# First block: two half-empty weight tiles joined, gate tiles moved behind the preparation, three pairs' logits between the last tiles

## What is computed

```python
h = rms_norm(x, g_pre)
a_q, a_kv, a_g, b_cq, b_ckv, b_kr, c_q, c_kv, z = split_cols(h @ w_in)
o_a = nsa_attention(a_q, a_kv, a_g, cmp_pos, cmp_w1, cmp_w2, rel_bias[:4])   # compressed, selected, window; gates a_g
q_full = concat(q_nope, rope(q_rope))  from  rms_norm(b_cq, q_norm) @ w_uq
k_full = concat(k_nope, rope(b_kr))    from  rms_norm(b_ckv, kv_norm) @ w_ukv
o_b = causal_block_attention(q_full, k_full, v)
o_c = banded_attention(c_q, c_k, c_v, 128, rel_bias[4:], sinks)
mixed = concat(o_a, o_b, o_c) * silu(z)
x = x + rms_norm(mixed @ w_out, g_post)
```

## Time and profile before

| | us |
|---|---|
| median of three runs (2575.82 to 2582.0) | 2581.92 |
| the profiled execution, its own time | 2581.8 |
| its span, first to last instruction | 2580.0 |
| first layer's tiles 6 to 23 with the preparation | 51.4 to 177.4 |
| second layer's tiles 6 to 23 with the preparation | 366.5 to 492.9 |

### The profile page before, as it was taken

How to read it: one execution, slowest core, us unless ns; L and a number is a source line. 1 busy time by engine, 2 the same in 40 slices (tenths; PEclk the granted TensorE clock), 3 DMA queues, 4 the chain that set the end, 5 groups by cost and what they waited for, 6 DMA issues and landing times. The chain is left out here.

```text
span 2580.0 us, 35090 instructions
## 1 busy us (share of the span) xinstructions
PE 2469.5 (96%) x13238; PEld 1980.9 (77%) x13238; DVE 1294.1 (50%) x1920; ACT 661.1 (26%) x1331; POOL 654.4 (25%) x510
## 2 busy tenths in 40 slices
PE   8999999999699999999999999899999999999997
PEld 6866778667588888788788888788887887788885
DVE  5547565574633343787533334433345776533344
ACT  3126330263211100643311100311102533311101
POOL 2005510164233311101433311333312002333311
PEclk9989999999899999999999999999999999999998
DMA  6400132000322322221222331222321312223322
GB/s 256 136 32 18 50 133 86 25 18 17 105 98 97 101 101 84 91 75 58 77 95 97 110 106 66 91 98 94 111 97 65 107 51 74 83 96 98 115 98 77
DMA packets 58666, 224.83 MB, mean 87 GB/s; under 512 B 6404, under 2 KB 8596, under 8 KB 58300
## 3 DMA queue, kind: packets, MB, share of 16 engines
q1 hardware_dynamic: 54288, 208.96, 24.5%
q10 hardware_dynamic: 4268, 14.33, 1.5%
HBM read 221.14 MB, written 5.80 MB: 88 GB/s over the span
## 5 line engine op out<-in xcount | busy, mean ns | idle before, releaser
L172 DVE CAST two_hi<-two_raw 128x1024 fp32r<-128x1024 f32 (+1 forms) x292 | 220.1, 754 | 900.0 <-PE bank L241 891.0
L234 PE MATMUL bank<-xh,two_hi 128*128 128x512 f32 x1728 | 429.8, 391 | 0.2 <-ACT up_sg L1570 0.2
L241 PE MATMUL bank<-xl,two_hi 128*128 128x512 f32 x1728 | 428.2, 390 | 0.0
L237 PE MATMUL bank<-xh,two_lo 128*128 128x512 f32 x1728 | 426.8, 389 | 0.0
L174 DVE TENSOR_TENSOR two_lo<-two_raw,two_hi 128x1024 fp32r<-128x1024 f32 (+1 forms) x292 | 400.9, 1373 | 10.0
L241 PEld LDWEIGHTS bank<-xl,two_hi 128*128 128x128 f32 x1728 | 324.9, 188 | 67.5
L237 PEld LDWEIGHTS bank<-xh,two_lo 128*128 128x128 f32 x1728 | 324.4, 188 | 67.5
L234 PEld LDWEIGHTS bank<-xh,two_hi 128*128 128x128 f32 x1728 | 322.9, 188 | 68.8 <-issue 1.6
L1591 POOL TENSOR_TENSOR up_hm<-up_sg,up_hm 128x512 f32<-128x512 f32 x88 | 197.5, 2244 | 554.7 <-ACT up_hm L1573 554.7
L234 PE MATMUL bank<-hh,two_hi 128*128 128x512 f32 x704 | 171.8, 392 | 0.0
L241 PE MATMUL bank<-hl,two_hi 128*128 128x512 f32 x704 | 171.4, 390 | 0.0
(11 more groups left out here) (287 smaller groups left out, 2947.8 us busy)
## 6 DMA issues: line engine op xcount, KB each, us to landing
two_raw<-in_up SPq DMA_DIRECT2D x180, 512.0 KB, 3.3
two_raw<-in_down SPq DMA_DIRECT2D x64, 704.0 KB, 4.0
one_raw<-in_w_in SPq DMA_DIRECT2D x48, 512.0 KB, 3.4
two_raw<-in_w_in SPq DMA_DIRECT2D x40, 512.0 KB, 3.3
one_raw<-in_w_out SPq DMA_DIRECT2D x16, 512.0 KB, 3.3
two_raw<-in_w_out SPq DMA_DIRECT2D x16, 512.0 KB, 3.6
w<-in_w ACTq DMA_DIRECT2D x2, 2048.0 KB, 17.5
x<-in_x SPq DMA_DIRECT2D x4, 512.0 KB, 7.1
```

The source lines that it names most:

```text
L172: v.tensor_copy(st.hi[:, h, 0:w], st.raw[:, r, 0:w]).then_inc(st.hi_made, 1)
L234: pe.matmul(out[:], st.hi[:, slot, k * P:(k + 1) * P], xh[:, h * kp + k, :], start=h == 0 and k == 0, stop=False)
L237: pe.matmul(out[:], st.lo[:, slot, k * P:(k + 1) * P], xh[:, h * kp + k, :], start=False, stop=False)
L241: mm = pe.matmul(out[:], st.hi[:, slot, k * P:(k + 1) * P], xl[:, h * kp + k, :], start=False, stop=h == pieces - 1 and k == kp - 1)
```

## The change

`C_KC` and `C_GATE` become one tile, `T_KCG` (64 key channels, 12 gate channels, padding); `C_KSLC` and `C_KWIN` become one, `T_KSW`. A layer has 22 tiles, numbered by `T_...`, and `proj` keeps its 24 rows (`ROW_OF`). The eviction of a joined tile copies its channels to where they stood before: 3 instructions for `T_KCG`, 4 for `T_KSW`. The order is `T_KR`, `T_KCG`, 2 `T_CQ`, `T_CKV`, `T_CMP`, `T_V`, the 8 gate tiles, `T_KSW`, 2 `T_QA`, 4 `T_QC`. The preparation moves to the tiles 5 to 14. Silu of all gates stands in one piece on ACT behind `uv`, with the read of the two bias tables (first layer only) behind it. Steps 0, 1 and 2 of the attention stand behind the tiles 19, 20 and 21; their logits lie in `pt_ring` since `lg_ring` is still taken. The PSUM banks are given tile by tile.

```diff
+(T_KR, T_KCG, T_CQ, T_CKV, T_CMP, T_V, T_Z, T_KSW, T_QA, T_QC, N_IN) = (0, 1, 2, 4, 5, 6, 7, 15, 16, 18, 22)
-IN_BANKS = (0, 4, 1, 2, 6, 7)
+IN_BANKS = (0, 4, 1, 2, 6, 7) + (0, 4, 1, 2, 0, 4, 1, 2, 0, 1) + (4, 7, 4, 7, 4, 7)
+AHEAD = 3
 def last_in_bank(i):
-    return i - 6 if i < 10 else i - 4
+    return max((j for j in range(i) if IN_BANKS[j] == IN_BANKS[i]), default=-1)
+def split_first(v, st, n):
+    r, h = n % RAW_RING, n % HL_RING
+    v.wait_ge(st.w_loaded[r], (n // RAW_RING + 1) * 16)
+    v.wait_ge(st.mm_done, n + 1)
+    v.tensor_copy(st.hi[:, h, :], st.raw[:, r, :]).then_inc(st.hi_made, 1)
...
     def lg(i):
-        return kit.lg_ring[:, i % L_RING]
+        return pt_ring[:, i + 1] if i < AHEAD else kit.lg_ring[:, i % L_RING]
...
# scalar
+        a.wait_ge(s["taken"], T_Z + DC)
+        a.preload_act_table(ACT.Silu)
+        for c in range(DC):
+            a.activation(proj[:, C_Z + c, :], proj[:, C_Z + c, :], ACT.Silu).then_inc(s["z_made"], 1)
+        if l == 0:
+            begin["read_bias"](a)
+        a.preload_act_table_set(EXP_LN)
...
# vector, evict(i)
+            if i in (T_KCG, T_KSW):
+                low, high = slice(0, HD), slice(HD, P)
+                copies = (((low, C_KC, low), (low, C_KC, high), (slice(HD, HD + 12), C_GATE, slice(HD, HD + 12)))
+                          if i == T_KCG else
+                          ((low, C_KSLC, low), (low, C_KSLC, high), (high, C_KWIN, low), (high, C_KWIN, high)))
+                for n, (r, c, q) in enumerate(copies):
+                    out = v.tensor_tensor(proj[q, c, :], src[r, :], kit.xrstd[r, :], ALU.mult)
...
# vector, tile loop: rope keys 10 -> 5, tpe 17 -> 6, norms 18 -> 7, rope queries 20, 21 -> 9, 11,
# hidden step 21 -> 12, compressed keys and gates 23 -> 14
+            if i >= N_IN - AHEAD:
+                if i == N_IN - AHEAD:
+                    v.wait_ge(start["read_a"], 16)
+                    v.wait_ge(s["z_made"], DC)
+                step(i - N_IN + AHEAD)
+        for j in range(AHEAD, NU + WEIGH_LAG + 1):
...
# tensor, tile loop: transposes 12 -> 5 (the gates' with them), sums of squares 17 -> 6, compress 18, 20 -> 7, 10,
# uk 19 -> 8, up_queries 20, 21 -> 9, 11, second step and uv 22 -> 13, transposes of the values 23 -> 14
+            if i >= N_IN - AHEAD:
+                step(i - N_IN + AHEAD)
+        for j in range(AHEAD, NU + WEIGH_LAG):
             step(j)
```

More of the change, by code:

```diff
@@ L709, in scalar @@
         a.activation(kit.xrstd[:], kit.xrstd[:], ACT.Exp, scale=-0.5).then_inc(s["rstd_made"], 1)
[L710 to L718, removed]
+        a.wait_ge(s["g_turned"], 1)
         a.activation(cv[:], bank[5][:, 0:NT * HD].rearrange("p (n c) -> p n c", c=HD), ACT.Copy
                      ).then_inc(s["cv_kept"], 1)
-        for j, c in enumerate((C_CQ, C_CQ + 1, C_CKV)):
-            a.wait_ge(s["taken"], c + 1)
+        a.activation(ge[:], bank[5][:, 2 * P:2 * P + NT * 12].rearrange("p (n c) -> p n c", c=12), ACT.Exp,
+                     scale=-1.0).then_inc(s["gates"], 1)
+        for j, (t, c) in enumerate(((T_CQ, C_CQ), (T_CQ + 1, C_CQ + 1), (T_CKV, C_CKV))):
+            a.wait_ge(s["taken"], t + 1)
             a.activation(sq[:, j, :], proj[:, c, :], ACT.Square).then_inc(s["sq_made"], 1)
@@ L727, in scalar @@
             a.wait_ge(s["sq_summed"], j + 1)
-            a.activation(rq[j], bank[5 + j][:], ACT.Ln, bias=kit.eps[:, 0:1], scale=1.0 / width
+            a.activation(rq[j], bank[(5, 3)[j]][:], ACT.Ln, bias=kit.eps[:, 0:1], scale=1.0 / width
                          ).then_inc(s["qln_made"], 1)
@@ L882, in vector @@
                 evict(i)
-            if i == 10:
+            if i == 5:
                 v.wait_ge(s["s1_in"], 16)
@@ L1046, in tensor @@
         for i in range(2, N_IN):
-            if before and i < len(IN_BANKS):
+            if before and i < DC - 2:
                 pe.wait_ge(before["x_made"], i + 1)
@@ L1059, in tensor @@
                           ).then_inc(s["xsq_summed"], 1)
-            if i == 12:
+            if i == 5:
                 if l == 0:
                     pe.wait_ge(start["k1_in"], 16)
-                pe.wait_ge(s["taken"], C_KR + 1)
+                pe.wait_ge(s["taken"], T_KCG + 1)
                 for n in range(NT):
@@ L1067, in tensor @@
                 mm.then_inc(s["cv_turned"], 1)
-            if i == 17:
+                for n in range(NT):
+                    mm = pe.transpose(bank[5][:, 2 * P + n * 12:2 * P + (n + 1) * 12],
+                                      proj[HD:HD + 12, C_GATE, n * P:(n + 1) * P], ident[HD:HD + 12, HD:HD + 12])
+                mm.then_inc(s["g_turned"], 1)
+            if i == 6:
                 pe.wait_ge(s["cv_kept"], 1)
+                pe.wait_ge(s["gates"], 1)
                 pe.wait_ge(s["sq_made"], 2)
@@ L1100, in tensor @@
                           ).then_inc(s["cmp2_mm"], 1)
-                pe.wait_ge(s["taken"], C_GATE + 1)
-                for n in range(NT):
-                    mm = pe.transpose(bank[7][:, 2 * P + n * 12:2 * P + (n + 1) * 12],
-                                      proj[0:12, C_GATE, n * P:(n + 1) * P], ident[0:12, 0:12])
-                mm.then_inc(s["g_turned"], 1)
                 pe.wait_ge(s["qk_made"], 2 * B_HEADS)
```

105 lines of the change are left out of this document (53 added, 52 removed).

## The result

| | before | after |
|---|---|---|
| median, us (lowest to highest, 4 runs each) | 2581.9 (2575.82 to 2582.0) | 2554.32 (2552.61 to 2558.07) |
| the profiled execution, its own time | 2581.8 | 2555.51 |
| ratio, 95% interval | | 0.9901, 0.9882 to 0.992 |

The changed kernel is 27.6 us faster: 2554.3 against a forecast of 2550 and a range of 2543 to 2561. The first lines of the pages of before and after count the work that went: 96 products on TensorE (PE), as four tiles of 24 have them.

The account below looks back on a forecast made before the run. TensorE's own work was taken to bound the first block's tiles, with waits where the attention starts. Gains of 14.6 us (first layer) and 17.4 (second), together 32.0, from 2581.8 gave 2549.8, say 2550 us; range 2543 to 2561.

Parts of the forecast that it names:

- The tiles: Two tiles less in each layer: four of 5.44 us, 21.8 us gained, 10.9 in each layer.
- The waits gone: TensorE's waits at the end of each layer's tiles vanish: 2.8 us gained in the first layer, 3.6 in the second.
- The new wait: First layer, before the first compression: TensorE waits for VectorE, held up by the load of `s1`; 1.7 us lost.
- The clock at the start of the attention: Three pairs' logits between the last tiles remove slow clock and idle: 1.7 and 0.9 us first layer, 2.9 second.
- The falls in the preparation: The clock's fall behind the compression stays at the same price, 5.0 and 5.1 us in the two layers.
- The sign of being wrong that was named: Among the signs of a wrong forecast: a longer stretch below full clock between tiles 6 and 14.
- The second block has the same instructions: The attention's later steps, output products and second block keep the same instructions; the sum has no term for them.
- Only the tiles count: Rival: waits come back elsewhere, through VectorE's work or the attention's start; only 21.8 us remain, 2560; chance 0.14.
- A fall of its own: Rival: TensorE's new wait before the first compression lengthens or adds a clock fall, 1.7 to 3.4 us; 2553; chance 0.06.
- The landings decide: Rival: `s1` is only whole with `w1` at 63.1, first layer loses 6.1 us more; 2556; chance 0.08.
- The clock gives more: Rival: with small products a tile apart, clock falls behind the compression shrink to half; 2545; chance 0.10.
- Slower: the clock stays down: Rival: tiles 6 to 14 with the preparation run at mean clock 0.66, 62 us more, 2612; chance 0.02.

Follow-up runs that it names:

- the first experiment: The changed kernel with the attention's first three steps behind the last tile again in both layers (AHEAD = 0); 2550.8 us, ratio to before 0.9901.
- The second trace of before: The kernel before, nothing changed, executed once more for a trace; its own time 2573.9 us.
- The first trace: The kernel before, nothing changed, in the profiled execution that the prediction was read from; its own time 2581.8 us.

## Why the prediction was right, and where it was not

**The tiles: right.** 5.44 us each was said; the tiles 20 and 21 of the first experiment's kernel start 5.44 us apart (156.79 and 162.23), and four more tiles cost 21.5 us in the first block.

**The waits gone: right.** The second trace of before takes 311.2 us from the first layer's seventh pair to the second's (498.39 less 187.21), and the three of after take 296.8 to 297.0, with as much time at the lower clock in between (10.2 us in each). That is 14.2 to 14.4 gained; tiles of 10.9 and waits of 3.6, without the clock, made 14.5.

**The new wait: right in place and cause, about half in size.** It was put at 1.7 us and measured 1.08, 0.94 and 0.64. VectorE's chain ended at 67.4, as said (67.1), but TensorE came later than 65.6: it finished tile 7 at 66.4.

**The clock at the start of the attention: right in sign, wrong in cause and in size.** The terms 1.7, 0.9 and 2.9 were given to the three pairs' logits. These brought nothing; the start is free without them, and what is left as the reason is that the preparation no longer stands there. And they were priced by one execution: 0 and 0 us, 3.4 and 6.8 us, 0 and 6.8 us at the lower clock in the other three of before. The 0.9 from a shorter start didn't come either, 8.06 us in place of 8.1.

**The falls in the preparation: the step that failed.** "The clock's fall behind the compression stays, I take it, at the same price" took 5.0 and 5.1 us as a property of that place in the code. The four traces of before have 10.2, 0, 10.2 and 0 us of them in the first layer. The first trace was at the dear end, and so was the set's median of 2581.9. Against it the first block gained 32.2 us where I added up 32.0; against the usual 2575 the whole change is worth 19.4 us, not 27.6. That the number came out is in part luck. The first layer gained 1.4 us less than was said, 0.9 of it the shorter start that did not come. The second gained 2.4 more, as its preparation had 3.4 us at the lower clock and not the 10.2 that were to stay. And 2550 was counted from an execution of 2581.8; the same 32.0 taken from the usual 2575 end at 2543, the edge of the range and 11 us under the measured time. The sign of being wrong that was named, a longer stretch below full clock, was there in the first trace (10.2 us in one piece, where the longest before had 6.8), with the same sum. The Trainium skill, TensorE: Matmul & The Clock Gate, "HAM oscillation", lays falls to idle gaps between bursts of products; the waits of 1.25 and 0.84 us stand in a trace with no fall as well, so a price can't be hung on gaps of this length.

**"The second block has the same instructions": true, and yet 5.9 us were lost there.** They lie in another place in TensorE's program, which costs 2.8 to 4.1 us at one loop (10.16 to 11.54 less 7.4). Here the sum has no term, and the trace of before, with its stand of 7.40 us, gave no size for one. The other 1.8 us of the first trace are in small steps whose cause stays open.

**The rivals.** *Only the tiles count*: the order without the joining is worth 3.4 us in the medians, and the whole change against the usual before 19.4, so in size it was near the truth, but not by its mechanism: the waits went, and the second block's loop took 2.8 to 4.1 us back. *A fall of its own* named 2553 and the right wait; whether the fall of 10.2 us hangs on it stays open. *The landings decide*: `w1` was there in time. *The clock gives more*: the preparation of after has 3.4 to 10.2 us at the lower clock in each layer, that of before 0 to 10.2, so no shrinking can be told. *Slower: the clock stays down*: over 66 to 108 the mean clock of the changed kernel is 0.88 to 0.96 in its three traces.

## What to carry to other kernels

Count what is structural (products taken out, waits that end a chain) and keep falls of the clock out of the sum until several executions of the same code show them at the same place. Removing or adding instructions also moves all later code of that engine: when an unchanged loop gets slower by a fixed amount, move it with a few waits that are already met, and see. And of a change with several parts, take each out once: here one part (the logits between the tiles) brought nothing, and two lines in another order (small loads ahead of large copies) and 64 waits gave 8 us more.

## What the runs showed of the hardware

- At a loop's restart TensorE stood 7.4 to 7.6 or 10.2 to 11.5 us, by the place of its code; 33 instructions more ahead of it changed the long stand into the short one and 257 more did not. In the long stands a second 16 KB piece of instructions landed 1.3 to 1.5 us before the first product.
- The same instructions with the same waits ran from 0 to 20.5 us at 1.2 GHz in the two preparations together, from execution to execution; the second layer's seventh pair came between 498.4 and 508.6 us.
- A load of 0.9 MB issued on ScalarE's queue landed after 35.5 us behind the copies of the bias tables and after 6.8 us at most ahead of them.
